# Cross attention computed in two halves of two heads each, with the halves placed between the chunks of neighbouring products

## What is computed

```python
# within second_block, b = 1, s = 256, D_MODEL = 1024, XA_HEADS = 4, XA_HEAD_DIM = 256
x = x + jnp.concatenate([y_na, y_ml, y_gd], axis=-1) @ w_out[l]
x = x + memory_cross_attention(rmsnorm(x, norm_xa_w[l]), rmsnorm(mem, norm_mem_w[l]),
                               w_xq[l], w_xkv[l], w_xo[l])
h = rmsnorm(x, norm_ffn_w[l])
x = x + jnp.square(jax.nn.relu(h @ w_ff1[l])) @ w_ff2[l]
```

## Time and profile before

| | us |
|---|---|
| median of 3 runs | 1065.22 |
| lowest and highest run | 1064.44, 1067.38 |
| the profiled execution | 1064.96 |
| its span | 1063.2 |
| TensorE busy | 1018.5 (96%) |
| VectorE busy | 763.1 (72%) |
| ScalarE busy | 567.8 (53%) |
| GpSimd busy | 82.7 (8%) |

### The profile page before, as it was taken

One profiled execution on the slowest core, in us unless ns is written; L12 is line 12 of the kernel. 1 busy time (PEld: TensorE's weight loads), 2 busy tenths in 40 slices (PEclk: granted clock), 3 DMA queues, 4 the chain that ended last, 5 costly groups with the idle time before them and its releaser, 6 DMA issues.

```text
span 1063.2 us, 22055 instructions
## 1 busy us (share of the span) xinstructions
PE 1018.5 (96%) x9301; PEld 940.9 (88%) x9301; DVE 763.1 (72%) x1210; ACT 567.8 (53%) x832; POOL 82.7 (8%) x176
## 2 busy tenths in 40 slices
PE   7999999999999999999898998789999999999996
PEld 6878999999878999999898998779799799998885
DVE  6879677788867786688889786756677656555445
ACT  5775485444765566543466664125345456665332
POOL 8500000010000000033520000000000000000000
PEclk9999999999999999999999999899999999999999
DMA  9645554484655544469575440001355256565652
GB/s 314 181 135 160 141 160 118 142 266 160 212 144 161 159 139 131 128 174 206 187 202 143 123 139 24 23 23 45 117 173 185 80 167 185 166 194 183 194 184 75
DMA packets 72210, 160.59 MB, mean 151 GB/s; under 512 B 6853, under 2 KB 13184, under 8 KB 72112
## 3 DMA queue, kind: packets, MB, share of 16 engines
q1 hardware_dynamic: 68960, 150.59, 46.6%
q0 software_dynamic: 2832, 8.06, 3.3%
q10 hardware_dynamic: 320, 0.53, 0.1%
HBM read 158.11 MB, written 1.05 MB: 150 GB/s over the span
## 4 chain that ended last, share of the span: by engine, by line
PE 86%; DVE 7%; ACT 3%; issue 2%; DMA 1%; SPq 0%; ACTq 0%; DVEq 0%
PE psum L464 23%; PE psum L466 22%; PE psum L465 22%; DVE ring_lo L1332 2%; PE psum L850 2%; PE psum L999 2%; PE psum L839 1%; PE psum L691 1%; PE psum L669 1%; DMA ring<-in_w_out 1%; DVE arena L1735 1%; PE psum L1285 1%; PE psum L1272 1%; DVE arena L1492 1%; PE psum L683 1%
## 5 line engine op out<-in xcount | busy, mean ns | idle before, releaser
L1332 DVE TENSOR_TENSOR ring_lo<-ring,ring_hi 128x1024 fp32r<-128x1024 f32 (+4 forms) x288 | 351.0, 1235 | 183.9 <-ACT ring_hi L2320 181.3
L2320 ACT ACTIVATE ring_hi<-ring 128x1024 fp32r<-128x1024 f32 (+4 forms) x288 | 298.2, 1045 | 287.7 <-PE psum L466 265.2
L464 PE MATMUL psum<-hT,ring_hi 128*128 128x256 f32 x904 | 259.2, 287 | 5.4 <-DVE ring_lo L1332 2.7
L466 PE MATMUL psum<-hT,ring_lo 128*128 128x256 f32 x904 | 256.2, 283 | 0.0
L465 PE MATMUL psum<-hT,ring_hi 128*128 128x256 f32 x904 | 255.9, 283 | 0.0
L464 PEld LDWEIGHTS psum<-hT,ring_hi 128*128 128x128 f32 x904 | 173.0, 191 | 8.3 <-issue 7.8
L464 PE MATMUL psum<-ring_hi,hT 128*128 128x512 f32 (+3 forms) x480 | 168.0, 350 | 6.3 <-DVE arena L1726 3.3
L466 PEld LDWEIGHTS psum<-hT,ring_lo 128*128 128x128 f32 x904 | 173.1, 191 | 0.0
L465 PEld LDWEIGHTS psum<-hT,ring_hi 128*128 128x128 f32 x904 | 173.1, 191 | 0.0
L466 PE MATMUL psum<-ring_hi,hT 128*128 128x512 f32 (+3 forms) x480 | 163.9, 342 | 0.0
L465 PE MATMUL psum<-ring_lo,hT 128*128 128x512 f32 (+3 forms) x480 | 163.9, 341 | 0.0
(11 more groups left out here) (449 smaller groups left out, 1357.9 us busy)
## 6 DMA issues: line engine op xcount, KB each, us to landing
ring<-in_w_in SPq DMA_DIRECT2D x96, 512.0 KB, 3.6
ring<-in_w_ff SPq DMA_DIRECT2D x64, 512.0 KB, 3.6
ring<-in_w_branch SPq DMA_DIRECT2D x24, 512.0 KB, 4.3
ring<-in_w_out SPq DMA_DIRECT2D x24, 512.0 KB, 3.8
ring<-in_w_in SPq DMA_DIRECT2D x16, 520.0 KB, 3.7
ring<-in_w_xkv SPq DMA_DIRECT2D x16, 512.0 KB, 3.8
ring<-in_w_in SPq DMA_DIRECT2D x12, 384.0 KB, 3.3
ring<-in_w_in SPq DMA_DIRECT2D x8, 528.0 KB, 4.0
```

The source lines that it names most:

```text
L464: mm(b, lhs[0], rhs[0], start=start, stop=False, **how)
L466: return mm(b, lhs[1], rhs[0], start=False, stop=stop, **how)
L1332: V.tensor_tensor(chunk_view(ring_lo, RAW, c), chunk_view(ring, RAW, c), plain(chunk_view(ring_hi, RING_HI, c)), ALU.subtract).then_inc(ev ...
L2320: AC(chunk_view(ring_hi, RING_HI, c), chunk_view(ring, RAW, c), ACT.Copy).then_inc(ev("whi_ready"), 1)
```

## The change

The attention is cut by heads instead of by row tiles: half g is heads 2g and 2g+1, for both row tiles. Scores, softmax, turns and outputs each become a function of g. TensorE's order becomes: `xq` half 0, a first quarter of `xv` half 1, `squares_sum(3)`, scores of half 0, `xq` half 1, turns of half 0, a second quarter of `xv`, scores of half 1, outputs of half 0, the last two quarters of `xv`, turns of half 1, two chunks of `wxo`, outputs of half 1, the other six chunks of `wxo`. The list of weights follows, so that chunk 56 is now the first of `xv`, 57 to 60 are `xq` half 1, 61 to 63 the rest of `xv`. Each chunk of `wxo` waits for the low parts of the head that its rows belong to. `hi_until` and `lo_until` are placed anew. On VectorE the maxima of the two row tiles use separate columns of `smax`, the sums of both row tiles share one reciprocal and one product of 128 x 1024, and three instructions no longer wait for their own end (`vf` for `v`). The number of matmuls, columns and bytes is the same; there are four exponentials of 512 columns instead of two of 1024, and four sums of 512 instead of two of 1024.

```diff
@@ the list of weights @@
-        for i in range(2):
-            w_cols(A["w_xq_2"][0], BANK * i, BANK)
-        w_cols(A["w_xkv_2"][0], BANK * 3, BANK)
+        w_cols(A["w_xq_2"][0], 0, BANK)
+        w_cols(A["w_xkv_2"][0], BANK * 3, BANK, part=range(1))
+        w_cols(A["w_xq_2"][0], BANK, BANK)
+        w_cols(A["w_xkv_2"][0], BANK * 3, BANK, part=range(1, CHUNKS))
@@ TensorE @@
-            for i in range(2):
-                gemm_T(("xq", i), xaT, after={0: squares_sum(3)} if i else {})
-            copied(pe, *[(n, i, g) for n in ("xk", "xq") for i in range(2) for g in range(2)])
-            for t in range(T):
-                for g in range(2):
+            values = cols_steps(("xv", 1), hT)
+
+            def attention_scores(g):
+
+                copied(pe, *[(n, g, z) for n in ("xk", "xq") for z in range(2)])
+                for t in range(T):
...
-            gemm_cols(("xv", 1), hT)
-            for t in range(T):
-                pe.wait_ge(ev("xp_ready"), t + 1)
-                for g in range(2):
+            def attention_turns(g):
+
+                pe.wait_ge(ev("xp_ready"), g + 1)
+                for t in range(T):
                     turns(("xpT", t, g), [x_s[:, t, 2 * g + h, m_ * P:(m_ + 1) * P] for m_ in range(2) for h in range(2)])
-            copied(pe, *[("xpT", t, g) for t in range(T) for g in range(2)], *[("xv", i, t, 0) for i in range(2) for t in range(T)])
-            for h in range(XH):
...
-            pe.wait_ge(ev("lo_made"), SPLITS1 * DEPTH + 6 + XH)
-            gemm_rows_T(("wxo",), x_oT, KD, lambda k: None)
+            def attention_out(g):
+
+                copied(pe, *[("xpT", t, g) for t in range(T)], *[("xv", g, t, 0) for t in range(T)])
+                for h in (2 * g, 2 * g + 1):
...
+            gemm_T(("xq", 0), xaT)
+            next(values)
+            squares_sum(3)()
+            attention_scores(0)
+            gemm_T(("xq", 1), xaT)
+            attention_turns(0)
+            next(values)
+            attention_scores(1)
+            attention_out(0)
+            next(values)
+            run(values)
+            attention_turns(1)
+            mixed = rows_T_steps(("wxo",), x_oT, KD, lambda k: pe.wait_ge(ev("lo_made"), SPLITS1 * DEPTH + 6 + (k // 2 + 1 if k < 6 else XH)))
+            next(mixed)
+            next(mixed)
+            attention_out(1)
+            run(mixed)
@@ VectorE @@
-            lo_until(61)
+            lo_until(59)
             rms(3)
...
-            lo_until(64)
+            lo_until(60)
             attention_maxima(0, 0)
+            attention_maxima(1, 0)
+            lo_until(62)
+            attention_parts(0)
+            lo_until(65)
             attention_maxima(0, 1)
-            attention_maxima(1, 0)
             attention_maxima(1, 1)
-            attention_parts(0)
             attention_parts(1)
-            lo_until(68)
-            for h in range(XH):
...
+            attention_low(0)
+            lo_until(69)
+            attention_low(1)
             lo_until(74)
@@ ScalarE @@
-            hi_until(63)
...
+            hi_until(61)
+            attention_exp(0)
+            hi_until(64)
+            copy_out(("xq", 1, 0), xq_T[:, 4:6, :], BANK, shape=2)
+            copy_out(("xq", 1, 1), xq_T[:, 6:8, :], BANK, shape=2)
+            attention_turned(0)
+            hi_until(65)
+            attention_exp(1)
+            attention_high(0)
+            hi_until(66)
+            memory_v(1)
             hi_until(68)
-            for h in range(XH):
-                high(("xo", h), x_oT[:, 0, 2 * h:2 * h + 2, :], 2)
+            attention_turned(1)
+            hi_until(69)
+            attention_high(1)
             hi_until(74)
```

More of the change, by code:

```diff
@@ L371, in build, with w_cols @@
         lo_at = {}
-        def w_cols(w, c0, n, more=False):
+        def w_cols(w, c0, n, more=False, part=range(CHUNKS)):
             rows_ = KD // CHUNKS
-            for c in range(CHUNKS):
+            for c in part:
                 src = w[c * rows_ * P:(c + 1) * rows_ * P, c0:c0 + n].rearrange("(k p) n -> p k n", p=P)
@@ L1273, in _ @@
                     filled(m, ("xs", t, g))
-            gemm_cols(("xv", 1), hT)
-            for t in range(T):
-                pe.wait_ge(ev("xp_ready"), t + 1)
-                for g in range(2):
+            def attention_turns(g):
+                pe.wait_ge(ev("xp_ready"), g + 1)
+                for t in range(T):
                     turns(("xpT", t, g), [x_s[:, t, 2 * g + h, m_ * P:(m_ + 1) * P] for m_ in range(2) for h in range(2)])
-            copied(pe, *[("xpT", t, g) for t in range(T) for g in range(2)], *[("xv", i, t, 0) for i in range(2) for t in range(T)])
-            for h in range(XH):
-                b = open_bank(pe, ("xo", h))
-                for e in range(2):
-                    for k in range(2):
-                        c = h * XD + e * P
-                        m = mm(b[:, e * S:(e + 1) * S], x_v[:, k, c:c + P], x_pT[:, k, h, :], start=(k == 0), stop=(k == 1))
-                filled(m, ("xo", h))
-            pe.wait_ge(ev("lo_made"), SPLITS1 * DEPTH + 6 + XH)
-            gemm_rows_T(("wxo",), x_oT, KD, lambda k: None)
+            def attention_out(g):
+                copied(pe, *[("xpT", t, g) for t in range(T)], *[("xv", g, t, 0) for t in range(T)])
+                for h in (2 * g, 2 * g + 1):
+                    b = open_bank(pe, ("xo", h))
+                    for e in range(2):
+                        for k in range(2):
+                            c = h * XD + e * P
+                            m = mm(b[:, e * S:(e + 1) * S], x_v[:, k, c:c + P], x_pT[:, k, h, :], start=(k == 0), stop=(k == 1))
+                    filled(m, ("xo", h))
+            gemm_T(("xq", 0), xaT)
[15 more added lines that the diff above has]
+            run(mixed)
             def x_rows():
@@ L2745, in _, with attention_exp, attention_turned @@
             copy_out(("xq", 0, 1), xq_T[:, 2:4, :], BANK, shape=2)
-            hi_until(63)
-            copy_out(("xq", 1, 0), xq_T[:, 4:6, :], BANK, shape=2)
-            copy_out(("xq", 1, 1), xq_T[:, 6:8, :], BANK, shape=2)
-            hi_until(64)
-            for t in range(T):
-                copied(act, ("xs", t, 0), ("xs", t, 1))
-                act.wait_ge(ev("xs_scale"), 1)
-                s1 = x_s[:, t, :, :].rearrange("p h n -> p (h n)")
-                af(AC(s1, s1, ACT.Exp, scale=rx_more[:, t:t + 1]), "xe_ready")
-            hi_until(67)
-            memory_v(1)
-            for t in range(T):
-                for g in range(2):
+            def attention_exp(g):
+                act.wait_ge(ev("xs_scale"), 1)
+                for t in range(T):
+                    copied(act, ("xs", t, g))
+                    s1 = x_s[:, t, 2 * g:2 * g + 2, :].rearrange("p h n -> p (h n)")
+                    af(AC(s1, s1, ACT.Exp, scale=rx_more[:, t:t + 1]), "xe_ready")
+            def attention_turned(g):
+                for t in range(T):
                     n = ("xpT", t, g)
@@ L2761, in _, with attention_high @@
                     af(AC(x_pT[:, :, 2 * g:2 * g + 2, t * P:(t + 1) * P], b, ACT.Copy), free(n))
+            def attention_high(g):
+                for h in (2 * g, 2 * g + 1):
+                    high(("xo", h), x_oT[:, 0, 2 * h:2 * h + 2, :], 2)
+            hi_until(61)
[9 more added lines that the diff above has]
+            memory_v(1)
             hi_until(68)
-            for h in range(XH):
-                high(("xo", h), x_oT[:, 0, 2 * h:2 * h + 2, :], 2)
+            attention_turned(1)
+            hi_until(69)
+            attention_high(1)
             hi_until(74)
```

22 lines of the change are left out of this document (13 added, 9 removed).

## The result

The changed kernel took 1061.38 us as the median of 8 executions (1054.37 to 1062.53), the kernel before 1066.00 in 8 beside it (1064.44 to 1067.38). The ratio is 0.9946, 95% interval 0.9926 to 0.9966: faster, by 5.7 us with 3.6 to 7.9. The profiled execution took 1061.13 us with a span of 1059.4.

What follows compares the result with a forecast made beforehand. TensorE, busy 96% of the span, bounds the kernel, so only its waits or clock can give time. 4.16 - 0.38 - 0.16 = 3.62 us won, 1065.22 - 3.6 = 1061.6 us; range 1060.3 to 1064.6.

Steps and rivals of the forecast that it cites:

- Which waits go: TensorE's waits before scores (1.05 us), outputs (1.25) and `wxo` (1.86) vanish, together 4.16 us.
- The walk: New program laid on the old trace's clock, engine by engine: stage ends near 868.3 instead of 871.9.
- Returns from fp32 work: On TensorE, products behind fp32 work are followed late: five such returns, 0.75 us, instead of three, 0.37.
- +0.38: Net TensorE time added by more returns from fp32 work, in us; bounds +0.03 to +0.58.
- The new wait for bank 3: `wxo` waits for ScalarE's copy of `xv` out of bank 3: +0.16 us, between 0 and 0.3.
- Rival A: Softmax of half 0 late, TensorE waits at first turns: 1 us gives 1062.6, 3 us 1064.6; chance 0.25.
- Rival B: Chunk 61's weights land late and hold up half 0's softmax: 1067.6 at 8 us behind; chance 0.06.
- Rival C: The three waits return under other names because bank-emptying engines pace the stage: 1065.2, with returns 1065.6; chance 0.06.
- The range: Whole-kernel time from 1060.3 to 1064.6 us, the top being A with 3 us of waiting.
- the split of the chance: Of the forecast's 0.62, 0.53 counted as faster, 0.09 as the same, around a 3.2 us detection line.

Runs made afterwards that it cites:

- place a: Both kernels with 16 fulfilled waits on TensorE and four memsets on VectorE added at the start: changed 0.9973, before's work 0.9991, against the kernel before.
- d: Both kernels with 60 fulfilled waits on TensorE added at the start, no memsets: changed 0.9933, before's work 0.9987, against the kernel before.
- the pairs: Before's and changed work compared untouched and with four different additions of waits or memsets at the start: gains 5.5, 2.2, 3.7, 4.0 and 5.3 us.

## Why the prediction was right and wrong

- **Which waits go, and that none comes back: right.** All three are gone, nothing replaces them, and the 191.36 us behind the stage give nothing back.
- **The walk: right in order, waits and pace.** On its own clock the program is 0.05 us ahead of it at scores 0 and 0.6 at the end; that the raw times agree within 0.3 us is the luck of a trace that runs 0.30 us later. Doubled scores show that TensorE alone sets the stage.
- **Returns from fp32 work: the price per return was right, the sum was not.** The five steps are 0.18, 0.09, 0.19, 0.10 and 0.19, together 0.75 as forecast. But the first product behind fp32 work also starts early (its row is 0.47 or 0.58 us long instead of 0.28 or 0.39), and each piece of fp32 work that a product follows has that. The four pieces of 16 rows are followed 3.35, 3.45, 3.26 and 3.26 us after their starts, together 13.32, where two pieces of 32 rows at 6.79 each make 13.58: 0.26 less. The term "+0.38" counted what a return costs and not what goes with it.
- **The new wait for bank 3: right in kind, smaller.** The turns of half 1 are followed after 0.86 us, those of half 0 after 0.79, so the wait is 0.07 for 0.16 (0 to 0.3 had been the bounds). Both together take 1.65 with this wait in it, where the walk had 16 steps of 0.109, 1.75, and the 0.16 beside them: 0.10 less than the steps alone. Put right, the sum is 4.16 - 0.38 + 0.26 + 0.10 = 4.14, as measured. So the terms 0.38 and 0.16, 0.54 together, were in effect 0.02. These are the mis-sized terms of the sum: 0.5 us of the 2.1 by which the gain came out larger than the 3.6 of the forecast. The bounds of 3.3 to 4.1 just hold the 4.14.
- **Rival A, the softmax late: it did not happen, and the margin is measured twice**, 2.5 us in the trace and 2.6 by taking it away. The exponentials cost 0.12 us more than taken, the other steps less. (That no low part lay between in the old order is a misreading: one of 1.22 us ran at 819.89, ahead of the maxima.) A's prices were too low, though: I gave 1 us of waiting 1 us of time, and where TensorE stood still for 2.7 or 3.1 us the clock took another 1.5 to 1.8.
- **Rival B, chunk 61 late:** its high part started at 817.00 without waiting for a transfer. **Rival C:** refuted by the empty wait list.
- **The range: wrong, and this is the step that failed.** Its low end was the largest gain less 0.8 us, "by which the lowest run lies under the median" of three runs. Eight executions of the changed kernel spread over 1054.37 to 1062.53 us, and moving the instructions of the same work shifts its mean by up to 3.6 us against the kernel before on the same chip (2.8 us under it at place a, 6.4 at d). By the pairs, a gain of 4.1 in the traces can show as 2.2 to 5.5. The sum did not break the range: put right it gives 1065.2 - 4.1 = 1061.1, inside. The 0.8 us did, where 1.6 were measured beyond the traces' gain. A low end of 1065.2 - 4.1 - 2 = 1059.1, with 2 us for that scatter, would have held the 1059.5; the 2 us are chosen with the result in hand. Likewise the split of the chance at a line 0.4 us from the forecast rested on a difference smaller than what the place of the program adds or takes.

No run beat the changed kernel by design. The copy with 60 idle waits is faster (0.9933), but its stage is the same, 58.75 us long, so what it wins is outside the stage.

## What to carry to other kernels

Walk the new order on the old trace's clock, engine by engine: when the work itself is unchanged, such a walk can hold to about half a microsecond (0.6 of 87 here), and it tells which margin each cover has. Compare the two traces from a point ahead of all that changed, or an offset between them hides or feigns an error. When a piece of fp32 work is cut in several, take the time of a piece from start to next start in a row of that size, not as a share of the long one. And judge a gain of a few microseconds in a millisecond by the stage's length in traces, or over several placements of the same program: one comparison, however tight its interval, can also measure where the instructions came to lie.

## What the runs showed of the hardware

- TensorE standing still for 2.7 and 3.1 us brought the granted clock to 0.83 and 0.85 over the next 10 us and cost 1.5 to 1.8 us on top; idle times of 0.89, 1.10 and 1.51 us cost no clock.
- A product of 256 or 512 columns behind fp32 matmuls is followed 0.18 or 0.19 us late, one behind fp32 transposes 0.09 or 0.10, and it starts early by about as much: its row is 0.47 or 0.58 us long behind fp32 matmuls where 0.28 or 0.39 is usual.
- With 60 fulfilled waits at the start of the program, some 600 to 750 us ahead, TensorE's waits for issue at short 64 x 64 products came to 0.7 and 0.8 us in two traces, for 4.1 to 5.7 in eleven without them. Why is open.
- An exponential of 128 x 512 with a scale for each partition takes 0.72 us, a copy of the same width from PSUM 0.60.
